# Compress stage of a hybrid decoder step: the first product over pairs of positions of one head, in two column groups

## The chip, the cores and the metric

The kernel runs on one core of one Trainium2 chip. The metric is the device time in microseconds (us) of one execution, from launch to the last output. The five engines of the core run programs of their own and meet at semaphores: TensorE (PE, its weight loads PEld), VectorE (DVE), ScalarE (ACT), GpSimd (POOL) and SyncE (SP), which here only issues DMAs.

## The reference, cut to what matters

One inference step of a one-layer decoder, for a prompt of 1024 tokens and 8 sequences that each add one token to 1024 cached ones. The part at issue is the compression of keys and values in the sparse attention heads. Cached raw keys and values lie in pages of 128 tokens, two heads of 64 elements side by side in a row of 128 numbers; a page table says which 8 pages a sequence has. Every block of 32 tokens of one head is flattened to 2048 numbers and goes through a small network:

```python
def compress(rows, pe, w1, w2):
    b, l, h, d = rows.shape
    nc = l // CMP_BLOCK                       # CMP_BLOCK = 32
    blocks = rows.reshape(b, nc, CMP_BLOCK, h, d) + pe[None, None, :, None, :]
    flat = blocks.transpose(0, 1, 3, 2, 4).reshape(b, nc, h, CMP_BLOCK * d)
    return jax.nn.silu(flat @ w1) @ w2        # w1 (2048, 64), w2 (64, 64)
```

It is done for keys and for values, over the 8 cached sequences (32 blocks each) and over the prompt (32 blocks), so over 9 x 32 = 288 blocks a head. The compressed keys are then normed. All is in float32.

## The kernel before

Four stages follow one another, with a barrier of all engines between them (`between`): `project` (input projection in 8 groups of columns, retention heads), `compress`, `attend_prompt`, `finish` (the 8 sequences and the output projection). A stage starts when every engine has left the one before. Inside a stage each engine's order of work is written out by hand; semaphores are counted, and nothing is planned at run time.

`project` works through column groups in the order qr, kr, vr, zr, q, wg, kv, zn, each for 8 tiles of 128 prompt rows and one tile of the 8 sample rows. Three pieces of it serve `compress`. In group kv, PE transposes the raw keys and values of each tile (L972) and DVE copies them to `kct` (L722), two of each a tile. In group zn, SP loads the 32 key pages of sequences 0 to 3 (L352) into `raw_a`. And SP loads the position vectors as single numbers, turned, into `pet` (L310, four DMAs).

`compress` (L1116 to L1378) goes through 16 units u: keys of sequences 0 to 7, then values. A unit is 8 pages, [128 tokens x 128] each. For each half unit i (4 pages), PE does 4 transposes of 128x128 into one of three PSUM banks (`turn_half`, L1328), after which head and element lie on the partitions and the token on the free axis. One copy of [128 x 512] then brings the half unit into `kcs` (`evacuate`, L1268 on DVE; for i = 1, 3, 5, 7 L1226 on ACT). It reads the bank in order and writes `kcs[:, position, block]` so that neighbouring numbers land 289 numbers apart. The page buffers are eight slots; SP issues pages 0 to 2, ACT pages 3 and 4, POOL pages 5 to 7 of each unit (L1163), values' pages after the keys' transposes have freed the slot.

The first product (`first`, L1347) is a sum over the 32 positions of a block: for each position one matmul with stationary weights of 128x128 (the 64x64 piece of w1 twice, for the two heads, on the diagonal, zeros elsewhere; DVE and POOL write the zeros, L1297 and L1204) and the moving columns of `kcs`. It runs in four parts: keys and values, each in a half of 128 columns (sequences 0 to 3) and a half of 161 (sequences 4 to 7, 32 blocks of the prompt, one column for the position vectors). Between every four positions PE turns one half unit of what is needed later. The prompt's columns come from `kct` by one DVE copy (L1257). Then come Silu on ACT (L1237), the second product (L1357), the key norms on DVE and POOL, and the transposes of the compressed keys (L1365).

Of the kernel before, what the change touches and what calls it, by code (L numbers as in the profile page):

```python
# [15 lines left out]
ACT = mybir.ActivationFunctionType  # L16
# [5 lines left out]
P = 128  # L22
D = 1024
T = 1024
# [109 lines left out]
def layout(nc, s):  # L134
# [21 lines left out]
    s.kct = m.put("kct", [P, 2, T])  # L156
# [17 lines left out]
    s.pet = tail.put("pe_t", [P, 2, CB])  # L174
    s.raw_a = Memory(nc, s.w_region).put("raw_pages_a", [P, FIRST, PAGES, P])
    s.c_first = [nc.alloc_semaphore(name=f"c_first{u}") for u in range(FIRST)]
# [11 lines left out]
def project(nc, s, io):  # L188
# [50 lines left out]
    with ExitStack() as ctx:  # L239
# [34 lines left out]
        def _(sp):  # L274
# [12 lines left out]

            load_x(0)
# [19 lines left out]
            for kv, pe_dram in enumerate((io["cmp_pe_k"], io["cmp_pe_v"])):  # L308
                for half in range(2):
                    sp.dma_start(pet[HD * half:HD * half + HD, kv, :],  # L310
                                 dram(pe_dram, 0, [1, HD], [HD, 32]),
                                 allow_slow_non_contiguous=True).then_inc(tables_in, 16)
            sp.dma_start(s.pages[:], io["page_table"].rearrange("(a b) p -> a (b p)", a=1)).then_inc(table_in, 16)
            for g in range(NG):
                if 1 <= g < NG - 1:
                    load_w(g + 1)
                for t in range(NT):
# [22 lines left out]
                    if kind == "zr":  # L340
                        sp.wait_ge(y_ready, t + 1)
                        to = io["y"][r0:r0 + n, 512:1024] if t < TT else dram(io["scratch"], O_ZR, [512, B], [1, 512])
                        sp.dma_start(to, s.st[0:n, slot, :]).then_inc(st_stored[slot], 16)
                    if kind == "zn" and t < 2 * FIRST:
                        if t == 0:
                            sp.wait_ge(table_in, 16)
                            sp.wait_ge(w_low, KT * (g + 1))
                        pool = io["cache_cmp_k"].rearrange("n t h d -> n t (h d)")
                        for p in range(4 * (t % 2), 4 * (t % 2) + 4):
                            at = PAGES * (t // 2) + p  # L350
                            page = sp.value_load(s.pages[0:1, at:at + 1], min_val=0, max_val=N_PHYS - 1)
                            sp.dma_start(s.raw_a[:, t // 2, p, :], pool[bass.ds(page, 1), :, :].rearrange("a t c -> (a t) c")).then_inc(s.c_first[t // 2], 16)  # L352
# [91 lines left out]
        turns_before = lambda kind, t: {"q": 2 * t, "wg": 2 * NT + t, "kv": 3 * NT + 2 * t}[kind]  # L444

        @block.scalar
        def _(act):
# [64 lines left out]
            def post(i):  # L512
# [4 lines left out]
                if kind in ("wg", "kv"):  # L517
                    br = 1 if kind == "wg" else 0
                    act.wait_ge(k_turned, b + (1 if kind == "wg" else 2))
# [91 lines left out]
        def _(dve):  # L611
# [100 lines left out]
            def post(i):  # L712
# [4 lines left out]
                if kind in ("wg", "kv"):  # L717
                    br = 1 if kind == "wg" else 0
                    if kind == "kv" and t < TT:
                        dve.wait_ge(k_turned, turns_before(kind, t) + 1)  # L720
                        for j in range(2):
                            own.step(nc.vector.tensor_copy(  # L722
                                view(s.kct[:, j, 4 * t:4 * t + 1], [1, 4], [32, 32]), view(s.ps[:, 3, P * j:P * j + 1], [32, 4], [1, 32])))
                        own.sync()
# [65 lines left out]
            for g in range(NG):  # L790
                for t in range(NT):
# [15 lines left out]
                    if i == 2 * NT:  # L807
                        dve.wait_ge(tables_in, 128)
# [39 lines left out]
        def _(pe):  # L848
# [103 lines left out]
            def post(i):  # L952
# [17 lines left out]
                if kind == "kv":  # L970
                    for j in range(2):
                        last = nc.tensor.transpose(s.ps[:, 3, P * j:P * j + n], st[:, KVW * j:KVW * j + KVW], one)  # L972
                    last.then_inc(k_turned, 1)
# [114 lines left out]
SLOTS, FIRST = 8, 4  # L1088
SP_PAGES, ACT_PAGES, POOL_PAGES = range(0, 3), range(3, 5), range(5, 8)

# [25 lines left out]
def compress(nc, s, io):  # L1116

    m = Memory(nc, s.x_region)
    w1 = m.put("w1_blocks", [P, 2, CB, P])
    raw_b = m.put("raw_pages_b", [P, SLOTS - FIRST, PAGES, P])  # L1120
# [9 lines left out]
    kcs = Memory(nc, s.w_region + 4 * FIRST * PAGES * P).put("kcs", [P, CB, ALL])  # L1130
    assert s.w_region + 4 * FIRST * PAGES * P + 4 * CB * ALL <= SB_END
    by_act = (1, 3, 5, 7)
    kept_a = lambda n: sum(1 for i in range(n) if i in by_act)
    kept_v = lambda n: n - kept_a(n)
    raw = lambda u: s.raw_a[:, u % SLOTS, :, :] if u % SLOTS < FIRST else raw_b[:, u % SLOTS - FIRST, :, :]
    pool_dram = [c.rearrange("n t h d -> n t (h d)") for c in (io["cache_cmp_k"], io["cache_cmp_v"])]
    with ExitStack() as ctx:
        sem = s.semaphore
        raw_in = [sem(f"c_raw_in{b}") for b in range(SLOTS)]
        raw_in_pool = [sem(f"c_raw_in_pool{b}") for b in range(SLOTS)]  # L1140
        w1_in, w2_in, zeroed = [sem(f"c_w1_in{kv}") for kv in range(2)], sem("c_w2_in"), sem("c_zeroed")
        cleared = sem("c_cleared")
        short_set, short_in, prompt_kept = sem("c_short_set"), sem("c_short_in"), sem("c_prompt_kept")
# [6 lines left out]

        OUT_BANK = [6, 7, 3]
# [4 lines left out]
        def load_pages(engine, u, some, loaded):  # L1156

            kv, b = u // B, u % B
            if u >= SLOTS:
                engine.wait_ge(turned, 2 * (u - SLOTS + 1))  # L1160
            for p in some:
                page = engine.value_load(s.pages[0:1, PAGES * b + p:PAGES * b + p + 1], min_val=0, max_val=N_PHYS - 1)
                engine.dma_start(raw(u)[:, p, :], pool_dram[kv][bass.ds(page, 1), :, :].rearrange("a t c -> (a t) c")).then_inc(loaded[u % SLOTS], 16)  # L1163

        def load_w1(engine, kv, half):
            at = slice(HD * half, HD * half + HD)
            engine.dma_start(w1[at, kv, :, HD * half:HD * half + HD],
# [1404 lines left out]
```

## Time and profile before

| | us |
|---|---|
| median of 3 runs | 987.76 (985.49, 987.76, 988.01) |
| span of the profiled execution, first to last instruction | 983.7 |
| the profiled execution's own time | not recorded; the median of the runs is 4.1 above the span |

| engine | busy us | share of the span | instructions |
|---|---|---|---|
| PE | 926.9 | 94% | 5293 |
| PEld | 705.9 | 72% | 5293 |
| DVE | 504.9 | 51% | 1079 |
| ACT | 314.3 | 32% | 699 |
| POOL | 191.3 | 19% | 235 |

`compress` runs from 486.6 to about 555.7 us of the span. Matmuls are pipelined, and the duration of a PE row holds the time through the array, so neighbouring rows overlap: the rate is read from start to start. One float32 matmul is two records in the trace, a transpose one.

### The profile page before, as it was taken

What the parts mean: (1) busy time and instruction counts of PE and PEld (TensorE: products, weight loads), DVE (VectorE), ACT (ScalarE), POOL (GpSimd) and SP (SyncE); (2) the same over time, 40 slices, a digit from 0 to 9 for tenths busy, and PEclk for the clock granted to TensorE, in tenths of its full rate; (3) what the DMA queues carried; (4) which work ended last, traced back from release to release, by engine and by line L of the source; (5) the groups of instructions that cost most, each with busy time, mean ns of one, the idle gap of its engine ahead of it and who ended that gap; (6) DMA issues with size and microseconds to landing.
All of it is one profiled execution on the core that took longest, in us unless ns stands there. A gap on an engine that the chain in (4) does not pass through costs nothing. (4 is left out here: it accounts for less than half of the span.)

```text
span 983.7 us, 15654 instructions
## 1 busy us (share of the span) xinstructions
PE 926.9 (94%) x5293; PEld 705.9 (72%) x5293; DVE 504.9 (51%) x1079; ACT 314.3 (32%) x699; POOL 191.3 (19%) x235
## 2 busy tenths in 40 slices
PE   7999989999999989999879998999999998999998
PEld 6676769998878777778579775666666665667784
DVE  4774253346344665450156357776666754564522
ACT  4222031223132334242110255555655553311100
POOL 1222222333102221110053102111011012343000
PEclk8999999999999999999979869999999999999999
DMA  7305811000621021312495410000000006788631
GB/s 263 132 17 117 213 42 46 2 1 1 233 115 49 22 65 47 106 43 94 114 207 154 104 47 22 22 22 22 1 22 1 22 18 219 225 224 294 207 103 48
DMA packets 90894, 91.13 MB, mean 93 GB/s; under 512 B 27630, under 2 KB 69534, under 8 KB 90454
## 3 DMA queue, kind: packets, MB, share of 16 engines
q1 hardware_dynamic: 70402, 71.60, 24.1%
q10 hardware_dynamic: 16700, 9.36, 3.5%
q0 software_dynamic: 3712, 9.17, 3.2%
q8 instruction: 43, 0.70, 0.3%
q14 instruction: 37, 0.30, 0.1%
HBM read 75.51 MB, written 23.49 MB: 101 GB/s over the span
## 5 line engine op out<-in xcount | busy, mean ns | idle before, releaser
L887 PE MATMUL ps<-w_high,x_high 128*128 128x512 f32 (+1 forms) x520 | 204.6, 393 | 2.3 <-DVE w_low L618 2.3
L889 PE MATMUL ps<-w_high,x_low 128*128 128x512 f32 (+1 forms) x520 | 199.8, 384 | 0.0
L888 PE MATMUL ps<-w_low,x_high 128*128 128x512 f32 (+1 forms) x520 | 199.3, 383 | 0.0
L887 PEld LDWEIGHTS ps<-w_high,x_high 128*128 128x128 f32 x520 | 98.1, 189 | 33.9 <-issue 12.9
L889 PEld LDWEIGHTS ps<-w_high,x_low 128*128 128x128 f32 x520 | 97.7, 188 | 20.9
L888 PEld LDWEIGHTS ps<-w_low,x_high 128*128 128x128 f32 x520 | 98.0, 188 | 18.9
L1718 PE MATMUL ps<-k_high,q_stack 128*128 128x512 f32 (+3 forms) x192 | 77.3, 406 | 12.1 <-DVE a_stats L1603 11.9
L399 POOL TENSOR_TENSOR stats<-stats,small 128x8 f32<-128x8 f32 (+3 forms) x35 | 41.7, 1190 | 213.9 <-DVE stats L670 159.3
L1718 PEld LDWEIGHTS ps<-k_high,q_stack 128*128 128x128 f32 x192 | 38.4, 200 | 53.2 <-DVE a_stats L1603 27.9
L1760 PE MATMUL ps<-weights_turned,v_nat 128*64 128x512 f32 x264 | 71.4, 622 | 0.0
L1719 PE MATMUL ps<-k_low,q_stack 128*128 128x512 f32 (+3 forms) x192 | 66.6, 354 | 0.0
L1268 DVE COPY kcs<-ps 128x512 f32<-128x512 f32 x28 | 30.3, 1084 | 62.6 <-PE ps L1328 62.5
L1512 POOL TENSOR_TENSOR y_tile<-y_tile,branch_out 128x512 f32<-128x512 f32 x15 | 19.1, 1276 | 221.5 <-DVEq L1661 221.5
L1603 DVE CUSTOM_DVE_ANT_1 window_logits<-ps,bias_full 128x640 f32<-128x640 f32 (+3 forms) x56 | 39.1, 709 | 34.0 <-PE ps L1719 33.7
L1533 ACT ACTIVATE full_logits<-full_logits,a_stats 128x128 f32<-128x128 f32 (+7 forms) x64 | 49.3, 771 | 20.8 <-DVE a_stats L1603 20.6
L1631 DVE COPY weights_turned<-ps 128x512 f32<-128x512 f32 x66 | 45.6, 690 | 18.8 <-PE ps L1739 14.3
L2359 PE MATMUL ps<-w_out_high,y_high 128*128 128x512 f32 x128 | 53.8, 420 | 1.4 <-DVE w_out_low L2086 1.4
L1542 ACT ACTIVATE weights_turned<-ps 128x512 f32<-128x512 f32 x66 | 39.0, 591 | 47.0 <-PE ps L1739 47.0
L456 ACT ACTIVATE w_high<-w_raw 128x512 fp32r<-128x512 f32 (+1 forms) x64 | 36.1, 601 | 54.6 <-PE ps L889 53.1
L1603 DVE CUSTOM_DVE_ANT_1 full_logits<-ps,bias_full 128x256 f32<-128x256 f32 (+6 forms) x56 | 45.0, 822 | 15.7 <-PE ps L1719 14.6
L2361 PE MATMUL ps<-w_out_high,y_low 128*128 128x512 f32 x128 | 50.2, 392 | 0.0
L2360 PE MATMUL ps<-w_out_low,y_high 128*128 128x512 f32 x128 | 50.0, 391 | 0.0
(340 smaller groups left out, 1597.9 us busy)
## 6 DMA issues: line engine op xcount, KB each, us to landing
w_raw<-in_w_in SPq DMA_DIRECT2D x48, 256.0 KB, 4.4
tmp_skew<-tmp_table SPq DMA_DIRECT2D x8, 576.0 KB
bias_full<-tmp_skew SPq DMA_DIRECT2D x8, 512.0 KB, 5.0
w_out_raw<-in_w_out SPq DMA_DIRECT2D x16, 256.0 KB, 4.7
y_rows_in<-tmp_y SPq DMA_DIRECT2D x8, 512.0 KB, 4.5
x_rows<-in_x_prompt SPq DMA_DIRECT2D x8, 512.0 KB, 5.6
out_y_prompt<-out_rows SPq DMA_DIRECT2D x8, 512.0 KB, 5.4
x_tile<-in_x_prompt SPq DMA_DIRECT2D x6, 512.0 KB, 3.9
```

The source lines that it names most:

```text
L887: nc.tensor.matmul(out, s.xh[:, k, rows], s.wh[:, k, 0:w], start=(k == 0), stop=False)
L888: nc.tensor.matmul(out, s.xh[:, k, rows], s.wl[:, k, 0:w], start=False, stop=False)
L889: ins = nc.tensor.matmul(out, s.xl[:, k, rows], s.wh[:, k, 0:w], start=False, stop=(k == KT - 1))
L1533: nc.scalar.activation(lg[:, h, 0:P * n], lg[:, h, 0:P * n], ACT.Exp, scale=-1.0, bias=st[:, S_MIN + H * j + h:S_MIN + H * j + h + 1], acc ...
L1603: nc.vector.tensor_tensor_reduce(out=columns(lg[:, h, 0:1]), in0=columns(pair[:, 0:1]), in1=view(full[:, TT - n, h, 0:1], [H * P, n], [1, ...
L1631: nc.vector.tensor_copy(pt[:, k % RP, 1, :], bank(k, 1)).then_inc(taken_v, 1)
L1718: nc.tensor.matmul(out, q(h), s.kh[:, j, h // G, k0 + c:k0 + c + w], start=True, stop=False)
L1719: last = nc.tensor.matmul(out, q(h), s.kl[:, j, h // G, k0 + c:k0 + c + w], start=False, stop=not (masked and c == 0))
L1760: last = nc.tensor.matmul(s.ps[at, 6, :], s.v[:, j, t + 1 - n + b, at], pt[:, k % RP, kv, :], start=(b == 0), stop=(b == n - 1))
L2359: nc.tensor.matmul(to, yh[:, t % 2, k, 0:n], wh[:, k, cols], start=(k == 0), stop=False)
L2360: nc.tensor.matmul(to, yh[:, t % 2, k, 0:n], wl[:, k, cols], start=False, stop=False)
L2361: last = nc.tensor.matmul(to, yl[:, t % 2, k, 0:n], wh[:, k, cols], start=False, stop=(k == KT - 1))
```

## The change

- Pages are loaded as pairs of tokens: one page goes to 64 partitions (a pair each) with 256 numbers a partition; two pages share a tile (`load_pages_paired`). A transpose of 128 columns then gives, for the even or the odd tokens, head and element on the partitions.
- A half unit i is now the even (i even) or odd tokens of a unit, and still 4 transposes. Its bank is brought to `kcs` by two copies of [64 x 512], one a head, that gather with steps of 16 numbers from PSUM and write runs of 32 neighbouring numbers. `kcs` has (parity, element) on its partitions, then head, pair of positions, block.
- The first product is over 16 pairs of positions: stationary weights 128x64 (`w1` as it is, no zeros to write), once for each head, the two heads' results in two column groups (PSUM partitions 0 to 63 and 64 to 127).
- The prompt is a ninth sequence (unit 8 and 17): its rows are read back from the output tensors by one DMA of 512 KB for the keys and one for the values. `kct`, its transposes and its copies go.
- The PSUM ring has four banks instead of three. DVE copies the half units 0 to 15 alone; from 16 on, ACT takes the odd ones. PE turns a whole unit after every three pairs of positions.
- Every unit from 6 on has a page buffer of its own. The pages of units 4 and 5 are loaded in `project`, in group q, into the place of `kct`. In `compress` 80 pages are loaded instead of 96. ACT issues all of its 20 pages before its first copy.
- The second product of the keys also waits for every copy (its banks are now in the ring).

```diff
+def load_pages_paired(engine, s, pool, b, some, tile, loaded):
+    for p in some:
+        page = engine.value_load(s.pages[0:1, PAGES * b + p:PAGES * b + p + 1], min_val=0, max_val=N_PHYS - 1)
+        at = HD * (p % 2)
+        engine.dma_start(tile[at:at + HD, p // 2, :], pool[bass.ds(page, 1), :, :].rearrange("a (r two) c -> (a r) (two c)", two=2)).then_inc(loaded, 16)
... (project)
+                    if kind == "q" and t < 2 * (EARLY - FIRST):
+                        if t == 0:
+                            sp.wait_ge(table_in, 16)
+                            sp.wait_ge(rows_in, 48)
+                            sp.wait_ge(r_out, TT)
+                        load_pages_paired(sp, s, pool, FIRST + t // 2, range(4 * (t % 2), 4 * (t % 2) + 4), s.raw_k[:, t // 2], s.c_first[FIRST + t // 2])
...
-                    for j in range(2):
-                        last = nc.tensor.transpose(s.ps[:, 3, P * j:P * j + n], st[:, KVW * j:KVW * j + KVW], one)
-                    last.then_inc(k_turned, 1)
... (compress)
-    w1 = m.put("w1_blocks", [P, 2, CB, P])
+    w1 = m.put("w1_pairs", [P, 2, CB // 2, HD])
-    by_act = (1, 3, 5, 7)
+    by_act = [i for i in range(4 * FIRST, 2 * n_u) if i % 2]
+        RING = 4
+        def load_prompt(engine, kv):
+            u = SEQS * kv + PROMPT
+            rows = io["prompt_out"][("cmp_k", "cmp_v")[kv]]
+            engine.wait_ge(turned, 2 * (kv + 1))
+            engine.dma_start(raw(u), dram(rows, 0, [2 * KVW, P], [2 * KVW * P, PAGES // 2], [1, 2 * KVW])).then_inc(raw_in[u], 16)
+        def kept_at(i, h):
+            b, at = i // 2 % SEQS, HD * (i % 2)
+            return kcs[at:at + HD, h, :, NBP * b:NBP * b + NBP]
+        def bank_of(i, h):
+            return view(s.ps[HD * h:HD * h + HD, i % RING, 0:1], [1, CB // 2], [CB // 2, NBP])
+        def may_keep(engine, i):
+            kv, b = i // 2 // SEQS, i // 2 % SEQS
+            if kv == 1:
+                engine.wait_ge(first_out, 1 if b < 4 else 2)
+            engine.wait_ge(turned, i + 1)
... (sync)
+            load_w1(sp, 0)
+            for u in paged[:2]:
+                load_pages(sp, u, SP_PAGES, raw_in)
+            load_prompt(sp, 0)
+            for u in paged[2:6]:
                 load_pages(sp, u, SP_PAGES, raw_in)
...
+            for u in paged[6:]:
                 load_pages(sp, u, SP_PAGES, raw_in)
+            load_prompt(sp, 1)
... (scalar)
+            for u in paged[:4]:
+                load_pages(act, u, ACT_PAGES, raw_in)
+            load_w1(act, 1)
+            for u in paged[4:]:
+                load_pages(act, u, ACT_PAGES, raw_in)
             for i in by_act:
+                may_keep(act, i)
+                for h in range(HKV):
+                    nc.scalar.activation(kept_at(i, h), bank_of(i, h), ACT.Copy).then_inc(evacuated_a, 1)
... (vector)
+            keep_position(0)
+            for i in range(2 * n_u):
+                if i == 2 * (SEQS + 4):
+                    keep_position(1)
+                if i not in by_act:
+                    may_keep(dve, i)
+                    for h in range(HKV):
+                        nc.vector.tensor_copy(kept_at(i, h), bank_of(i, h)).then_inc(evacuated, 1)
... (tensor)
+                for j in range(CB // 2):
+                    if then and j % 3 == 2:
+                        turn(then.pop(0))
+                    for h in range(HKV):
+                        last = nc.tensor.matmul(s.ps[HD * h:HD * h + HD, 4 + kv, cols], w1[:, kv, j, :], kcs[:, h, j, cols], start=(j == 0), stop=(j == CB // 2 - 1))
...
+            for u in range(FIRST):
+                turn(u)
+            first(0, 0, [4, 5, 6, 7, 8])
+            first(0, 1, [9, 10, 11, 12])
+            first(1, 0, [13, 14, 15, 16, 17])
+            second(0)
+            first(1, 1, [])
```

## Rows read from the trace of the kernel before

**Rows 1.** Busy time by stretch of compress: start:end length, engine (x instructions), clock, DMA share, GB/s
```profile
486.60:498.40 11.80, 5.91 (x36) 5.29 (x37) 8.28 (x8) 4.24 (x4) 5.59 (x9) 0.86 0.95 194
498.40:513.70 15.30, 12.06 (x94) 11.87 (x92) 8.71 (x8) 0.00 (x0) 9.16 (x13) 0.85 0.96 208
513.70:529.10 15.40, 15.15 (x96) 14.90 (x97) 8.83 (x10) 0.16 (x1) 7.57 (x14) 0.82 0.59 165
529.10:541.98 12.88, 11.74 (x103) 11.29 (x103) 9.49 (x11) 0.97 (x4) 2.81 (x6) 1.00 0.52 135
541.98:551.03 9.05, 9.05 (x67) 9.00 (x66) 2.55 (x12) 0.31 (x2) 2.09 (x3) 1.00 0.01 2
551.03:555.66 4.63, 2.93 (x16) 1.91 (x14) 1.68 (x6) 1.29 (x5) 0.01 (x1) 1.00 0.00 0
```

**Rows 2.** Timeline, PE in the first product: start, length, line, operation
```profile
504.98 0.60 PE L1328 MATMUL ps<-ident,raw_pages_b 128*128 128x128 f32 x4
505.41 1.06 PE L1347 MATMUL ps<-kcs,w_blocks 128*128 128x128 f32 x8
506.31 0.60 PE L1328 MATMUL ps<-ident,raw_pages_b 128*128 128x128 f32 x4
```

**Rows 3.** Waits in compress, PE for a DMA: total, times, longest
```profile
PE ps L1328 <- DMA raw_pages_a<-in_cache_cmp_v: 3.3, 1, 3.3
```

**Rows 4.** Timeline, PE in attend_prompt: two heads in two 64-wide column groups, and what follows
```profile
785.65 1.08 PE L1760 MATMUL ps<-weights_turned,v_nat 128*64 128x512 f32 x4
786.66 0.50 PE L1718 MATMUL ps<-k_high,q_stack 128*128 128x512 f32 x1
```

**Rows 5.** Groups of DVE instructions over the span, by shape: busy, mean ns, idle before
```profile
L1631 DVE COPY weights_turned<-ps 128x512 f32<-128x512 f32 x66 | 45.6, 690 | 18.8 <-PE ps L1739 14.3 <-DVE branch_out L1657 3.1 <-PE ps L1760 0.3
L1268 DVE COPY kcs<-ps 128x512 f32<-128x512 f32 x28 | 30.3, 1084 | 62.6 <-PE ps L1328 62.5
L2130 DVE TENSOR_REDUCE s_out_halves<-s_product 128x64 f32<-128x2048 f32 x1 | 3.7, 3731 | 0.0
```

**Rows 6.** Groups of ACT instructions over the span, by shape
```profile
L1542 ACT ACTIVATE weights_turned<-ps 128x512 f32<-128x512 f32 x66 | 39.0, 591 | 47.0 <-PE ps L1739 47.0
L510 ACT ACTIVATE q_stack<-ps,gain 128x512 fp32r<-128x512 f32 x16 | 10.2, 686 | 6.2 <-PE ps L962 6.1
L510 ACT ACTIVATE qfull<-ps,gain 64x32 f32<-64x32 f32 x2 | 0.6, 282 | 2.3 <-PE ps L988 2.3
L562 ACT ACTIVATE x_high<-ps 128x32 fp32r<-128x32 f32 x2 | 0.4, 198 | 6.5 <-PE ps L1001 6.4
L1226 ACT ACTIVATE kcs<-ps 128x512 f32<-128x512 f32 x4 | 4.2, 1113 | 9.5 <-issue 8.1 <-PE ps L1328 1.5
```

**Rows 7.** Timeline: four instructions back to back on DVE
```profile
843.15 2.49 DVE L2086 TENSOR_TENSOR w_out_low<-w_out_raw,w_out_high 128x512 fp32r<-128x512 f32 x4
```

**Rows 8.** Page loads of compress as issued by SP and ACT (timeline) and by POOL (by line)
```profile
518.73 12.82 SPq L1163 DMA_DIRECT2D raw_pages_b<-in_cache_cmp_v  x12
515.41 8.12 ACTq L1163 DMA_DIRECT2D raw_pages_b<-in_cache_cmp_v  x8
L1163 POOL DMA_DIRECT2D raw_pages_b<-in_cache_cmp_k x12: 547/547/954, 488.1 to 501.0; - x12
```

**Rows 9.** DMA issues from 486 to 560 us: KB each, median us from issue to landing
```profile
bias_full<-tmp_skew SPq DMA_DIRECT2D x6, 512.0 KB, 5.0
...
raw_pages_b<-in_cache_cmp_v SPq DMA_DIRECT2D x12, 64.0 KB, 2.3
```

**Rows 10.** Timeline, PE in group kv of project
```profile
407.61 0.38 PE L972 MATMUL ps<-ident,stage 128*128 128x128 f32 x2
407.83 0.38 PE L962 MATMUL ps<-ident,squares 128*128 128x128 f32 x2
```

**Rows 11.** Timeline, SP from 290 to 352 us: weight loads issued around group q
```profile
297.43 3.68 SPq L281 DMA_DIRECT2D w_raw<-in_w_in  x8
339.95 11.33 SPq L281 DMA_DIRECT2D w_raw<-in_w_in  x8
```

More of the change, by code:

```diff
@@ L518, in post @@
                     br = 1 if kind == "wg" else 0
[L519 removed]
+                    act.wait_ge(k_turned, b + 1)
                     if t < TT:
@@ L1156, in load_pages @@
         def load_pages(engine, u, some, loaded):
[L1158 to L1167, printed above, removed]
-                             dram(w1_dram[kv], 0, [HD, HD], [HD * HD, CB], [1, HD])).then_inc(w1_in[kv], 16)
@@ new lines, in turn @@
+            def turn(u):
+                landed(u)
+                for odd in range(2):
+                    i = 2 * u + odd
+                    if i >= RING:
+                        if i - RING in by_act:
+                            pe.wait_ge(evacuated_a, kept_a(i - RING + 1))
+                        else:
+                            pe.wait_ge(evacuated, kept_v(i - RING + 1))
+                    for q in range(PAGES // 2):
+                        last = nc.tensor.transpose(s.ps[:, i % RING, P * q:P * q + P], raw(u)[:, q, KVW * odd:KVW * odd + KVW], s.ident[:])
+                    last.then_inc(turned, 1)
@@ L1342, in first @@
-                pe.wait_ge(evacuated, kept_v(2 * B * kv + B * (half + 1)))
-                pe.wait_ge(evacuated_a, len(by_act))
-                for i in range(CB):
-                    if then and i % 4 == 0:
-                        turn_half(then + i // 4)
-                    last = nc.tensor.matmul(s.ps[:, 4 + kv, cols], w1[:, kv, i, :], kcs[:, i, cols], start=(i == 0), stop=(i == CB - 1))
+                    pe.wait_ge(w1_in[kv], 16)
+                else:
+                    pe.wait_ge(position_kept, kv + 1)
@@ L1366, in turn_keys @@
                 last.then_inc(key_turned, 1)
-            for i in range(B):
-                turn_half(i)
-            for kv in range(2):
-                for half in range(2):
-                    done = 2 * B * kv + B * (half + 1)
-                    first(kv, half, done if done < 4 * B else None)
-                    if kv == 1 and half == 0:
-                        second(0)
+            for u in range(FIRST):
[5 more added lines that the diff above has]
+            first(1, 1, [])
             turn_keys()
             second(1)
-            keep_clock(nc, s.ps[:, 0, 0:2 * P], w1[:, 1, 0, :], kcs[:, 0, 0:2 * P], 3)
+            keep_clock(nc, s.ps[:, 0, 0:2 * P], s.ident[:], kcs[:, 0, 0, 0:2 * P], 3)
 R_ = B * H
```

160 lines of the change are left out of this document (55 added, 105 removed).

## The prediction

> **What bounds the kernel now.** I read the table of stretches first, because the change touches one stage and a little of another. In compress, 486.6 to 555.7 us, PE is busy 57 of 69 us, DVE 40 [rows 1]. The stage falls into four kinds of time. At its start PE works half of the time and DVE, which copies what PE has turned, most of it: 8.3 of 11.8 us. Then PE works through products and transposes, with one gap waiting for pages, 3.3 us long [rows 3]. The reader is to see in [rows 1] that the two stretches around that gap have a mean clock of 0.85 and 0.82: PE fell to its lower level (1.2 of 2.4 GHz) behind each wait, and 15.4 us at 0.82 are 5.5 us at half speed, 2.8 us lost. From 514 us on PE is the bound: 15.2 of 15.4, 11.7 of 12.9, 9.05 of 9.05. Last comes a tail of 4.6 us of short dependent steps. A barrier ends the stage, so what the stage loses the run loses.
>
> **PE's prices.** A chunk of the timeline is four transposes from 504.98 to 505.41, 0.43 us, and four matmuls of 128 columns (eight records) to 506.31, 0.90 us [rows 2]: 0.225 us a matmul. With 161 columns it is 9.05 / 32 = 0.283 us [rows 1]. Before: 128 matmuls, 64 x 0.225 + 64 x 0.283 = 32.5 us, and 32 x 0.43 = 13.8 us of transposes.
>
> **Do two column groups of 64 run side by side?** The trace has that form: two heads, four records of 128x512 in 1.01 us, start to next start [rows 4]. At the rate of [rows 2] a record of 512 columns is 4 x 0.1125 = 0.45 us; one after another four make 1.80, side by side 0.90. So they run side by side, and 0.11 us is left. The products after are then 32 x 0.225 + 32 x 0.283 = 16.3 us; transposes 36 x 0.43 = 15.5 us. PE's sum falls by 14.5 us. I take the 0.11 as the price of going to the narrow form and back (bounds: 0, and 0.25 if all of the two latencies shows), 0.13 with a little for the wait of a transpose's data; there are 14 such returns, 1.8 us. The Trainium skill, TensorEngine Tiling (Array Packing), Key Properties, says that a change of tiling mode drains the array while a change of tile does not; the 0.11 us agrees with that, and at 14 returns it speaks against the change by under 2 us.
>
> **The copies.** Before: 32 copies of [128 x 512]. After: 72 of [64 x 512], 52 on DVE, 20 on ACT, each as long as one over 128 partitions. So the price of one decides the stage. The old copy takes 1084 ns on DVE and 1113 on ACT, where a copy of the same size with both sides in order takes 690 and 591 [rows 5, 6]: the scattered writing costs 400 to 520 ns. The new one writes in order and reads PSUM in steps of 16 numbers. No row of DVE shows such a read of PSUM. Lower bound 690 ns (L1631). Upper bound 1084: a DVE read of SBUF in steps of 64 costs 3731 ns for 2048 numbers [rows 5], 1.8 ns a number, just what the scatter costs. For ACT there is a row: L510 into `qfull` reads 32 numbers from PSUM in steps of 8, in 282 ns; a plain one takes 198 (L562), and the gain operand accounts for 686 - 591 = 95 [rows 6]. 198 + 95 = 293, so the step costs nothing there; at the scatter's 1.0 ns a number it would have shown 32 ns more. I take 690 on DVE too, as the same memory is read. Back to back four DVE instructions take 2.49 us, (2.49 - 0.69) / 3 = 0.60 each, 0.09 less than one alone [rows 7]. So I use 0.61 us a copy on DVE and 0.5 on ACT; at the other bound 1.0 on both.
>
> The Trainium skill, SBUF — State Buffer, Door 1: The DMA port swizzle, says that SBUF has lines of 16 bytes and PSUM of 8, that each access to a new line pays, and that any non-contiguous pattern in PSUM slows matmuls significantly. For SBUF the 1084 ns agree. For PSUM the ACT row does not, and for DVE nothing shows it; by the page the sum would be the first rival below.
>
> **The stage, step by step.**
> A. Start to first product. DVE alone copies half units 0 to 7: 487.3 + 0.2 (position column) + 16 x 0.61 = 497.4. Before: 498.4. The zero writing (3.5 us of DVE) is gone, and PE has four banks ahead, so nothing else is late.
> B. First product of the keys, first half. PE has only 16 x 0.225 + 5 x 0.86 + 0.65 = 8.6 us of work, but the next half waits for copies up to 17. DVE has 8 to 16: the first is ready at about 498.5, then 18 x 0.61 = 11.0; with 1 us for PE's transposes at the lower clock, 510.5. The copy of 17 is ACT's, which first issues 20 pages and a w1: 8 pages take 8.12 us [rows 8], so it is free at 488.5 + 21.1 = 509.6, done at 510.6. Before: 513.7. PE waits 2 us here in place of the 3.3 for pages, which are no longer reloaded into used slots.
> C. Second half. 16 x 0.283 + 4 x 0.86 + 4 x 0.13 = 8.5 us of PE, plus 2.4 for the lower clock behind the wait (2.8 before). DVE needs 1.22 and ACT 1.0 for what PE turns in 0.86 + 0.85, so PE leads. End 521.5, before 529.1.
> D. Values, first half. PE 8.6 us, to 530.1. But here the loads close in. SP's 12 pages take 12.82 us, POOL's 12.9 [rows 8]; 30 pages from 488.5 are 32 us, with 4 to 5 for the w1, w2 and prompt issues between, so the prompt's values are issued at 525. A DMA of 512 KB lands after 5.0 us [rows 9]: 530. Then 0.86 of transposes and 0.45 of product, and the last copies (0.2 + 1.2), for which the second product now waits: 532. Before: second product at 541.
> E. Second product 0.95, second half of the values 16 x 0.283 = 4.5: 537.5. The key norms, 4 us behind the second product, just fit. Before: 551.0.
> F. The tail is untouched, 4.6: 542.1 against 555.7.
> The stage gives back 13.5 us; I keep 13, for bubbles between turns that no row prices.
>
> **Project.** In group kv PE goes from matmul to matmul without a gap, and the two transposes L972 take 0.22 us of it, 407.61 to 407.83 [rows 10]: 8 x 0.22 and the two small ones, 1.8 us off the path. DVE's 16 copies of L722 go too; they lie beside PE and are worth nothing. Added are 16 page loads on SP in group q. SP has issued its weights by 301.1 and issues the next at 339.95 [rows 11]; 16 x 1.07 = 17 us fit. Its new waits are for work of the group before, and behind them stands only the weight load of 339.95; without that gap they would cost up to 17 us. Two position DMAs in place of four, half the w1 bytes: no one waits, 0.
>
> **Sum.** 983.7 - 13 - 1.8 = 968.9 of span, plus the 4.1 by which the median of the runs lies above the span: 973.
>
> **The rivals.**
> 1. The gather costs what the scatter did, on both engines. For: a step in SBUF does [rows 5]. Against: the ACT row, though of 32 numbers. A ends at 503.5, B at 523.7 (18 x 1.0), C at 534.6 or, if PE, which then works a third of the time, stays at the lower clock through it, at 541; D by DVE's five pairs of copies 10 us later, the last pair 2; E 5.5; F 4.6: 557 to 563. With -1.8 that is 987 to 993; as such waits lowered the clock each time before, I take 991: slower. It decides from about 0.95 us a copy.
> 2. DVE alone pays it. A and B are DVE's, so little is better: D is ACT's and PE's by half, end at 557, 987.
> 3. The narrow products run one after the other. B hides it, C is 4.5 later, D 2, E 4.5: +11, 984. Against it stand [rows 4].
> 4. Pages that go to 64 partitions, or the prompt rows, land late. From D on every us past 530 counts in full; a landing of 10 in place of 5 us makes 978. For: the DMA engines were at a share of 0.95 while three queues loaded pages [rows 1], and the 64 partitions may be reached by fewer of them. Against: a page landed in 2.3 us at the share of 0.5 to 0.6 that holds later [rows 9, 1], and it is now half as many pieces of twice the length.
> That a wider stall moves PE's clock in the next stage is within 3 us either way.
>
> **How the numbers follow.** Forecast 0.66 (968 to 978: gather 0.61 to 0.69 us, landings of 4 to 6, clock losses 0 to 3, the next stage), rival 1 0.11, rival 2 0.08, rival 3 0.04, rival 4 0.11. A difference under 0.3%, 3 us, can't be told from none. Faster: 0.66 + 0.11 + 0.02 of rival 3 + 0.02 of rival 2 = 0.81. Slower: 0.07 of rival 1. The same: 0.12. The range for 8 in 10 takes in rival 4 and reaches to rival 2: 967 to 987.
>
> **What would show it.** The copies at 0.69 (DVE) and 0.59 us (ACT), not near 1.1. Four product records of 128 columns in 0.225 us. Idle time of PE before the second half of the keys, released by a DVE or ACT copy, and before the last turn, released by the prompt's DMA. The stage 56 us long. In group kv two transposes fewer a tile. I am wrong if DVE's copies are over 0.9 us, if the stage is over 62 us, or if SP's later weight loads in project start after 341 us.

## The result and the profile after

Ten runs each: 981.48 us (978.74 to 984.75) in place of 986.48 (983.3 to 988.61). Ratio 0.9958, 95% interval 0.9940 to 0.9976: faster, by 5 us between the medians (4 by the ratio), where 14.8 were forecast. The profiled execution has a span of 981.5 us (before 983.7); its own time is 983.2, so a run takes 1.7 us more than its span. By that the profile of after lies 1.7 us above its median and the one of before 1.1 below its own, and the two spans differ by 2.2 only.

The table of stretches of compress, cut at the steps A to F of the prediction (PE, PEld, DVE, ACT, POOL busy, clock, DMA share, GB/s) [rows 1]:

```profile
489.13:501.85 12.72, 5.97 (x32) 5.10 (x33) 11.22 (x17) 0.00 (x0) 5.75 (x11) 0.77 0.79 197
501.85:518.70 16.85, 11.82 (x104) 9.20 (x105) 12.40 (x18) 1.20 (x2) 7.47 (x15) 0.80 0.85 195
518.70:530.10 11.40, 11.40 (x98) 9.02 (x98) 5.50 (x8) 4.80 (x8) 3.70 (x8) 0.80 0.33 95
530.10:541.27 11.17, 9.57 (x106) 7.66 (x105) 7.08 (x11) 6.67 (x12) 0.00 (x0) 1.00 0.61 161
541.27:546.75 5.48, 5.48 (x70) 4.93 (x71) 2.69 (x12) 0.77 (x3) 2.09 (x3) 1.00 0.01 3
546.75:551.95 5.20, 3.19 (x18) 2.11 (x16) 1.68 (x6) 1.29 (x5) 0.00 (x0) 1.00 0.01 2
```

The reader is to see two things. The stage starts at 489.13, 2.5 us later than before, though nothing of compress had begun. And the first two stretches, 29.6 us, have DVE busy for 23.6 and PE for 17.8, at a clock of 0.77 and 0.80; from 518.7 on PE is full. The stage takes 62.9 us in place of 69.0.

**Why it starts late.** First the end of project before, SP and ACT in the timeline, then the same after:

```profile
478.61 3.63 SPq L352 DMA_DIRECT2D raw_pages_a<-in_cache_cmp_k  x4
482.28 1.28 SPq L355 DMA_DIRECT2D tmp_zn<-stage  x2
...
482.61 0.59 ACT L475 ACTIVATE stage<-ps 8x512 f32<-8x512 f32 x1 [0.63 <-PE ps L879]
```

```profile
474.73 4.15 SPq L1090 DMA_DIRECT2D raw_pages_a<-in_cache_cmp_k  x4
478.92 0.58 SPq L356 DMA_DIRECT2D tmp_zn<-stage  x1
480.25 4.59 SPq L1090 DMA_DIRECT2D raw_pages_a<-in_cache_cmp_k  x4
484.89 0.99 SPq L356 DMA_DIRECT2D tmp_zn<-stage  x2
...
481.29 0.59 ACT L476 ACTIVATE stage<-ps 8x512 f32<-8x512 f32 x1 [1.51 <-DMA tmp_zn<-stage]
```

Before, SP issues a tile's pages and store in 4.86 us, and PE needs 5.55 a tile (ACT's copies are 5.55 apart); so SP, which starts group zn late, catches up, and its last store goes out as ACT's last copy ends. After, SP takes 5.52 us a tile (474.73 to 480.25): it never catches up, ACT waits 1.5 us for a store to land (before, its wait there was 0.63 us, and for PE), and the last two stores leave SP from 484.9 on. From the start of ACT's last copy to the next stage it is 7.8 us in place of 4.0.

**The copies.** The groups of compress, then DVE's timeline:

```profile
L1300 DVE COPY kcs<-ps 64x512 f32<-64x512 f32 x52 | 35.8, 689 | 14.3 <-PE ps L1333 13.0
...
L1245 ACT ACTIVATE kcs<-ps 64x512 f32<-64x512 f32 x20 | 12.0, 600 | 46.5 <-issue 35.5 <-PE ps L1333 10.8
```

```profile
490.25 11.50 DVE L1300 COPY kcs<-ps 64x512 f32<-64x512 f32 x16 [0.93 <-PE ps L1333]
504.06 12.97 DVE L1300 COPY kcs<-ps 64x512 f32<-64x512 f32 x18 [2.31 <-PE ps L1333]
```

689 and 600 ns, as long as a copy with both sides in order [rows 5, 6]: the read in steps is free. (The Trainium skill, SBUF — State Buffer, Door 1: The DMA port swizzle, gives PSUM lines of 8 bytes and says that a non-contiguous pattern there slows matmuls. For copies no such cost shows here: these read numbers 64 bytes apart and take as long as those in order.) But (11.50 - 0.69) / 15 = 0.72 us from start to start, not 0.61.

**The rest of the stage**, ACT and PE:

```profile
517.34 1.22 ACT L1245 ACTIVATE kcs<-ps 64x512 f32<-64x512 f32 x2 [35.46 <-issue]
...
518.70 1.34 PE L1350 MATMUL ps<-kcs,w_pairs 128*64 128x161 f32 x8 [4.69 <-ACT kcs L1245]
...
525.53 1.09 PE L1333 MATMUL ps<-ident,raw_pages_b 128*128 128x128 f32 x8
526.55 1.04 PE L1350 MATMUL ps<-kcs,w_pairs 128*64 128x161 f32 x12
527.52 1.09 PE L1333 MATMUL ps<-ident,raw_pages_b 128*128 128x128 f32 x8
...
541.27 1.02 PE L1362 MATMUL ps<-w_blocks,hidden 128*128 128x128 f32 x6 [1.60 <-ACT hidden L1250]
542.22 4.60 PE L1350 MATMUL ps<-kcs,w_pairs 128*64 128x161 f32 x64
```

ACT's first copy comes after its list of page loads, 1.5 us behind DVE's last (504.06 + 12.97 = 517.03), and PE waits 4.69 us. One load in that list is long, the first behind the DMA of `w1`; ACT's timeline from 500 to 503 us:

```profile
500.24 3.23 ACTq L1090 DMA_DIRECT2D raw_pages_b<-in_cache_cmp_v  x1
```

The median of ACT's page loads is 0.48 us. In the ten kernels below that keep this order it takes 2.0 to 3.1 us too.

A round of a turn and three pairs takes 525.53 to 527.52, 1.99 us; its parts alone are 0.86 + 3 x 0.283 = 1.71. The last half takes 4.5 us for 16 pairs, 0.283 each: the two heads run side by side.

### The profile page after: what moved, and what is told of

Same layout as the page of the kernel before. It is cut to its first block and busy times, and to the rows that moved or that the text cites. A ratio compares the mean times of both kernels' runs of the same rounds, so it can differ in the third digit from the quotient of the medians.

```text
span 981.5 us, 15674 instructions
## 1 busy us (share of the span) xinstructions
PE 915.1 (93%) x5291; PEld 686.9 (70%) x5291; DVE 501.2 (51%) x1083; ACT 321.9 (33%) x715; POOL 182.9 (19%) x227
## 5 line engine op out<-in xcount | busy, mean ns | idle before, releaser
L1537 ACT ACTIVATE window_logits<-window_logits,a_stats 128x640 f32<-128x640 f32 (+4 forms) x64 | 44.1, 689 | 18.4 <-DVE a_stats L1607 18.3
```

The costliest lines, as they stand in the source:

```text
L1537: nc.scalar.activation(lg[:, h, 0:P * n], lg[:, h, 0:P * n], ACT.Exp, scale=-1.0, bias=st[:, S_MIN + H * j + h:S_MIN + H * j + h + 1], acc ...
```

## The experiments

All are edits of the changed kernel. Medians are set against the kernel before on the same chip; kernels that ran once are read by their traces. Lengths of the stage run from its first transpose to attend_prompt's first matmul: 62.9 us in the changed kernel, and 61.4 to 62.9 in seven kernels whose stage is the same or came out the same (`plain_read`, `copy_as_scale`, `one_signal_a_pair`, `turned_order`, the two zn kernels, the changed kernel). So one trace tells lengths apart only beyond 1.5 us.

### Why compress starts late

```diff
# zn_old_form: group zn, SP
-load_pages_paired(sp, s, pool, t // 2, range(4 * (t % 2), 4 * (t % 2) + 4), s.raw_a[:, t // 2], ...)
+for p in range(4 * (t % 2), 4 * (t % 2) + 4):
...
+    sp.dma_start(s.raw_a[:, t // 2, p // 2, KVW * (p % 2):KVW * (p % 2) + KVW],
+                 pool[bass.ds(page, 1), :, :].rearrange("a t c -> (a t) c"))...
# zn_two_queues: SP keeps two pages a tile; the other two in POOL's loop
+if kind == "zn" and t < 2 * FIRST:
+    load_pages_paired(pool, s, cache_k, t // 2, range(4 * (t % 2) + 2, 4 * (t % 2) + 4), ...)
```

> Against the changed kernel only the 32 page loads in group zn of project differ: each goes to 128 partitions by 512 bytes again (the values of sequences 0 to 3 of the keys are then computed from wrongly placed rows). Theory A (the new form costs SP 468 ns an issue in place of 338 and its stores more as well, so SP and no longer PE sets the end of zn): an issue takes about 340 ns, the store 430, the last store leaves SP about 4 us earlier, compress starts at about 485.3 in place of 489.1, the run is about 4 us shorter than the changed kernel's 981.5 (977.5; 0.992 of the kernel before). Theory B (the start of compress came later for another reason, as DMA queues busy with the new lanes, or PE's clock): the issues get shorter but compress still starts at 488 to 489, and the time stays at 981.

> The changed kernel with the page loads of zn in the new form, but two of each tile's four issued by POOL, which has no work there. Theory A (SP's issue time is the bound): SP has 2 x about 1.04 + 0.6 us a tile, far below PE's 4.9; zn ends as PE allows, compress starts at about 485, the run at about 977.5 (0.992 of before). Theory B (the transfers themselves, into 64 partitions, hold up the weight or zn stores): same start as in the changed kernel, 489, time 981.

Measured: 975.97 us, ratio 0.9899 (0.9873 to 0.9925), and 976.48, 0.9897 (0.9872 to 0.9923). Compress starts at 482.8 and 484.95. SP in the first:

```profile
468.99 3.63 SPq L355 DMA_DIRECT2D raw_pages_a<-in_cache_cmp_k  x4
...
473.84 3.98 SPq L355 DMA_DIRECT2D raw_pages_a<-in_cache_cmp_k  x4
478.13 1.55 SPq L359 DMA_DIRECT2D tmp_zn<-stage  x2
```

and in the second:

```profile
470.00 1.72 SPq L1098 DMA_DIRECT2D raw_pages_a<-in_cache_cmp_k  x2
474.47 0.33 SPq L357 DMA_DIRECT2D tmp_zn<-stage  x1
475.55 1.71 SPq L1098 DMA_DIRECT2D raw_pages_a<-in_cache_cmp_k  x2
480.12 1.55 SPq L357 DMA_DIRECT2D tmp_zn<-stage  x2
```

4.85 us a tile of SP again, and in the second SP waits for PE's 5.55. From ACT's last copy to the next stage both have 4.1 to 4.2 us. In the eleven kernels with project as changed compress starts at 487.5 to 489.8 (mean 488.4), in the four with two queues at 483.0 to 485.0 (mean 483.8): 4.6 us. What lies ahead of group zn differs by over 2 us between executions, so it is cleaner to count from zn's first matmul to the first transpose of compress: 46.4 to 46.5 us in those eleven, 42.0 in the four with two queues, 41.8 in `zn_old_form` and in the kernel before. Theory A holds; the same bytes to the same 64 partitions in the second kernel rule out the transfers. So this alone took 4.5 to 4.7 us of what was forecast.

### The copies' distance, and which half of the partitions they touch

```diff
# plain_read: PSUM read in order
-return view(s.ps[HD * h:HD * h + HD, i % RING, 0:1], [1, CB // 2], [CB // 2, NBP])
+return view(s.ps[HD * h:HD * h + HD, i % RING, 0:1], [NBP, CB // 2], [1, NBP])
# copy_as_scale
-nc.vector.tensor_copy(kept_at(i, h), bank_of(i, h)).then_inc(evacuated, 1)
+nc.vector.tensor_scalar(kept_at(i, h), bank_of(i, h), 1.0, None, ALU.mult).then_inc(evacuated, 1)
# one_signal_a_pair: .then_inc(evacuated, 2) behind the second copy only
# same_partitions: read the half that is written
-s.ps[HD * h:HD * h + HD, i % RING, 0:1]
+s.ps[HD * (i % 2):HD * (i % 2) + HD, i % RING, 0:1]
# turned_order
-for h in range(HKV):
+for h in ((0, 1), (1, 0))[i % 2]:
```

> The changed kernel with the 72 copies of turned tokens reading PSUM in order in place of steps of 16 numbers (so each product takes the wrong columns). Theory A (the step is free; the 0.72 us from start to start is what any DVE instruction with a PSUM source takes back to back): mean 688 ns and 0.72 us apart as now, ACT 600 and 0.61, stage the same 62.9 us. Theory B (the step costs a little, hidden in the distance between starts): 16 copies in 9.8 us in place of 11.5, stretch A ends 1.7 us earlier, B about 2.

> The changed kernel with DVE's 52 copies written as a multiplication by 1.0 (TENSOR_SCALAR) in place of COPY; the result is the same. Theory A (COPY is what starts 0.72 us apart; two L829 TENSOR_TENSOR of 128x512 out of PSUM take 1.29 us together, 0.60 apart, in the same trace): 16 copies take 9.7 us in place of 11.5, A ends 1.8 and the second half of the keys starts about 1.5 to 2 us earlier (then ACT's copy of half unit 17, at 517.3, is the last); stage 1.5 to 2 us shorter, time about 979.5. Theory B (any one-source read of PSUM by 64 partitions, or the semaphore that each copy sets, gives 0.72): nothing changes, 981.5.

> The changed kernel with DVE signalling once behind each pair of copies in place of behind each copy; the result is the same. Theory A (the signal keeps the next copy from starting inside the last 0.1 us of the one before): pairs take 1.29 us in place of 1.41, the first copy of a pair no longer costs 0.72; 16 copies 10.6, stretch A 0.9 us shorter. Theory B (it lies in the access, not in the signal): 1.41 and 11.5 stay.

> The changed kernel with each DVE and ACT copy reading the same 64 partitions that it writes (so one head's products are computed from the other head's columns or its own twice). Theory A (0.72 us from start to start because a copy moves between partition halves, or because consecutive copies read different halves): 16 copies take 9.7 us in place of 11.5, stretch A 1.8 us shorter. Theory B (it lies elsewhere, in the signal after each copy or in the runs of 32 numbers that it writes): 0.72 stays.

> The changed kernel with DVE's two copies of each odd half unit in the other order (head 1 first). In stretch A successive pairs then read the same half of the partitions across the border of pairs and write another; inside a pair the half that is read changes and the half that is written does not, as before. The result is the same. Theory A (a change of the half read makes 0.72 us of 0.60, whatever is written): 16 copies take 0.69 + 8 x 0.72 + 7 x 0.60 = 10.65 us in place of 11.5. Theory B (a change of either half, read or written, does it): 11.5 stays.

Measured: `plain_read` 16 copies in 11.50 us; `copy_as_scale` 11.49, median 981.26, ratio 0.9949 (0.9933 to 0.9965), no gain over the changed kernel; `one_signal_a_pair` copies start at 490.91, 491.61, 492.33, 493.03, about 0.71 apart; `turned_order` 11.49. Only `same_partitions` moved. DVE's timeline there:

```profile
488.92 10.55 DVE L1300 COPY kcs<-ps 64x512 f32<-64x512 f32 x16 [0.93 <-PE ps L1333]
501.78 11.86 DVE L1300 COPY kcs<-ps 64x512 f32<-64x512 f32 x18 [2.31 <-PE ps L1333]
519.38 1.28 DVE L1300 COPY kcs<-ps 64x512 f32<-64x512 f32 x2 [5.74 <-PE ps L1333]
```

A pair takes 1.28 us in place of 1.41: 0.60 from start to start while both copies keep to one half of the partitions. From pair to pair the half changes, and 8 x 0.60 + 7 x 0.72 + 0.69 = 10.5 is just what 16 take. ACT's pairs fell from 1.22 to 1.08 too. `turned_order`, whose pairs meet on the half that is read but not on the one written, gained nothing, so a change of either side costs the 0.12 us. From pair to pair the PSUM bank changes too, and the copy has a wait in front of it, but neither makes the 0.12: two DVE instructions in project read two banks over all partitions, with a wait between them, and start 0.60 apart (timeline of the changed kernel):

```profile
157.60 1.29 DVE L829 TENSOR_TENSOR scores<-ps,decay 128x512 f32<-128x512 f32 x2
```

My first three theories (step, kind, signal) fell; `same_partitions` gave half of what its theory A expected (0.95 us of 1.8), as the change from pair to pair stayed; the last of the five was Theory B of its run. Against the 0.61 of the prediction this is an estimate of 34 x 0.11 = 3.7 us in A and B; no run has all its copies 0.60 apart. And as the copies stand each pair must change halves on the side it reads; another layout was not tried.

### ACT's late copy, its late Silu, and copies shared from the start

```diff
# w1_by_sp: load_w1(sp, 1) behind SP's 18th page in place of load_w1(act, 1)
# silu_early: in ACT's loop over by_act
+if i == 27:
+    hidden(0)
# share_from_start (w2 loads moved behind the prompt's values)
-by_act = [i for i in range(4 * FIRST, 2 * n_u) if i % 2]
+by_act = [1, 3, 5, 7] + [i for i in range(26, 2 * n_u) if i % 2]   # the first four ahead of ACT's loads
```

> The changed kernel with the load of w1 for the values issued by SP behind its first 18 pages in place of by ACT behind its first eight. Theory A (ACT's list of issues, 27.3 us, makes its copy of half unit 17 the last thing before the second half of the keys): ACT is free 0.9 to 1.3 us earlier, the copy ends at about 517.3 in place of 518.6, the second half starts with DVE's last copy, at 517.2 to 517.5; stage 1.2 us shorter. Theory B (ACT's issues wait on the DMA queues, not on their number): ACT's 20 page loads end at 517 all the same, under 0.3 us gained.

> The changed kernel with ACT's Silu of the keys ahead of its last five pairs of copies in place of behind them. Theory A: the second product no longer waits for hidden; it follows DVE's or ACT's last copy, idle time of PE ahead of it 0.8 to 0.9 in place of 1.6 us, stage 0.7 to 0.9 us shorter. Theory B (PE's transposes then wait for ACT's copies, which come 0.7 us later through the whole stretch): nothing gained.

> The changed kernel with ACT copying half units 1, 3, 5, 7 ahead of its page loads and DVE taking all of half units 8 to 25; w2 is loaded behind the prompt's values. Theory A (DVE's 0.72 us a copy bounds the first product of the keys): stretch A ends after 5.8 us of DVE in place of 11.5, about 496; DVE then ends half unit 17 at about 511 (before 518.7 with ACT's late copy), second half 522 to 523, the last prompt rows land near 531 to 534 and the second product starts at 535 to 536 in place of 541.3; stage end 546 to 547 in place of 552.0, time about 976 (0.990 to 0.991 of before). Theory B (PE's lower clock after the gaps, or landings of ACT's pages, which now start 5 us later, bound it): second product not before 539, gain under 2 us.

Measured: stage 61.8, 61.7 and 61.8 us, none of which can be told from no gain; `share_from_start` 980.74 us, 0.9947 (0.9927 to 0.9968), no better than the changed kernel. What moved shows inside the stage. In `w1_by_sp` the second half of the keys comes 27.95 us after the stage's start, now released by DVE; it is 29.57 in the changed kernel and 28.8 to 29.4 in seven others whose edit leaves that part alone. The longest of ACT's twenty loads is now 0.99 us. In `silu_early` the second product waits 1.02 us for a copy in place of 1.60 for `hidden`:

```profile
516.74 1.34 PE L1350 MATMUL ps<-kcs,w_pairs 128*64 128x161 f32 x8 [3.12 <-DVE kcs L1300]
```

```profile
538.76 1.02 PE L1368 MATMUL ps<-w_blocks,hidden 128*128 128x128 f32 x6 [1.02 <-ACT kcs L1253]
```

Both theories A hold for what PE waits for. The gains are some 1.2 us at the start of the second half, and 0.6 us of wait; that the stage keeps them shows only in `small_steps` below. Sharing the copies moved much and kept little:

```profile
496.25 0.66 PE L1355 MATMUL ps<-kcs,w_pairs 128*64 128x128 f32 x8 [1.78 <-ACT kcs L1241]
...
512.00 1.34 PE L1355 MATMUL ps<-kcs,w_pairs 128*64 128x161 f32 x8 [4.56 <-issue]
...
526.58 0.66 PE L1355 MATMUL ps<-kcs,w_pairs 128*64 128x128 f32 x8 [2.87 <-issue]
```

From the stage's start, A ends after 8.0 us (12.7 in the changed kernel) and B after 23.7 (29.6), as expected; but C takes 14.6 us in place of 11.4. Its clock is 0.55 in 510 to 515 us and 0.77 to 520, behind a wait of 4.6 us, and DVE, which has all of C's copies, is the last. Of 5.9 us won 3.2 go there, and D, at 0.75 in 525 to 530, takes 1.6 more. The second product starts at 539.3, as theory B said, and not at 535 to 536: behind the first half of the keys, theory A failed.

### The change of form, and the column groups

```diff
# turns_in_halves
-if then and j % 3 == 2:
-    turn(then.pop(0))
+if then and j % 3 == 1:
+    turn(then[0], (0,))
+if then and j % 3 == 2:
+    turn(then.pop(0), (1,))
# one_column_group
-last = nc.tensor.matmul(s.ps[HD * h:HD * h + HD, 4 + kv, cols], ...)
+at = 0 if j else HD * h
+last = nc.tensor.matmul(s.ps[at:at + HD, 4 + kv, cols], ...)
```

> The changed kernel with every turn inside a first product cut in two: half its transposes after position 1, half after position 2 of each three. Nothing is added but 14 more changes from 64-column to 128-column form and back. Theory A (each excursion costs PE 0.30 us in products and transposes): in the second half of the keys, where PE leads, four more excursions make 1.2 us, 11.4 to 12.6 us; a turn of four transposes and the four records behind it stand 0.15 above a plain row each. Theory B (it was not the change of form but waits for bank and pages): the stretch grows by under 0.4 us, and the two half turns together cost what one did.

> The changed kernel with both heads' products (from the second position on) sent to the same 64 columns of PE, so the sums of the two heads run together. Theory A (the two heads' records run side by side only since they go to different column groups): a pair of 161 columns takes 0.55 to 0.57 us in place of 0.283; the last product, 16 pairs in 4.60 us, takes 8.8; C 4.2 us longer, D 3.4 longer, B hides it behind the copies; stage 12 us longer, 994. Theory B (a 64-column product costs half by itself): the last product stays at 4.6 us.

Measured: with the turns in halves, a round at full clock, PE's timeline:

```profile
524.41 0.77 PE L1353 MATMUL ps<-kcs,w_pairs 128*64 128x161 f32 x8
525.11 0.66 PE L1334 MATMUL ps<-ident,raw_pages_b 128*128 128x128 f32 x4
525.69 0.49 PE L1353 MATMUL ps<-kcs,w_pairs 128*64 128x161 f32 x4
526.12 0.66 PE L1334 MATMUL ps<-ident,raw_pages_b 128*128 128x128 f32 x4
526.71 0.77 PE L1353 MATMUL ps<-kcs,w_pairs 128*64 128x161 f32 x8
```

524.41 to 526.71 is 2.30 us, against 1.99: 0.3 us for one excursion more, and C and D together take 25.6 in place of 22.6, 3.0 for nine more. Theory A holds: an excursion costs 0.3 us. (The Trainium skill, TensorEngine Tiling (Array Packing), Key Properties, says that a change of tiling mode drains the array. The trace agrees, and the price of 0.3 us is the trace's.) With one column group the last half:

```profile
543.95 8.69 PE L1351 MATMUL ps<-kcs,w_pairs 128*64 128x161 f32 x64
```

8.6 us to the next start in place of 4.5: theory A on the form. The stage is 70.3 us, 7.4 longer, not 12: C and D grew by 4.5 only, where 7.6 were expected, and A and B were 1.2 shorter. Part of it is the clock. The wait before C was short, and PE ran C at full clock, where the changed kernel has 0.80:

```profile
515.88 1.00 PE L1351 MATMUL ps<-kcs,w_pairs 128*64 128x161 f32 x8 [1.30 <-DVE kcs L1300]
```

```profile
515.88:530.00 14.12, 14.12 (x106) 12.34 (x107) 5.70 (x9) 4.80 (x8) 4.36 (x9) 1.00 0.33 94
```

The 11.4 us of C at 0.80 are 2.3 us lost, so about 2 of the missing 3.1 are a clock loss that this kernel does not have. The rest is open.

### Versions with the losses taken out

```diff
# small_steps = zn_two_queues + w1_by_sp + silu_early
# balanced = zn_two_queues + silu_early, and
+by_act = [i for i in range(2 * n_u) if i % 2]
+for i in (1, 3, 5, 7):
+    keep(i)
+for u in paged[:2]:
+    load_pages(act, u, ACT_PAGES, raw_in)
+for k in range(2, 10):
+    keep(2 * k + 5)
+    load_pages(act, paged[k], ACT_PAGES, raw_in)      # page loads: SP 33, ACT 14, POOL 33
# balanced_loads: the same, SP 30, ACT 19, POOL 31, w1 of the values by SP
```

> The changed kernel with zn's page loads on two queues, and in compress ACT copying every odd half unit from the start with its 14 page loads between the copies (SP and POOL 33 each), the prompt's values ahead of the last three sequences, w2 last, the Silu early. Theory A (copies are DVE's bound only while ACT issues loads; PE and the page issues are the floor): A 6 to 7 us, B 11, C 9.5 to 10.5, second product at about stage start + 47 (now + 52.1), stage end 57 us after its start in place of 62.9; with zn's 5 us the run is 971 (0.985 of before). Theory B (gaps that PE has between A and B lower its clock, and what A and B give, C loses, as when the copies were shared at the start alone): stage 60 to 61 us, run 974 to 975 (0.988).

> The changed kernel with three steps that each alone did what was expected: zn's page loads on two queues, w1 of the values loaded by SP, Silu of the keys early. If they add: compress starts at about 484.3, is 62.9 - 1.2 - 0.8 = 60.9 us long; the run is 4.3 + 2 = 6.3 us shorter than the changed kernel's, 975 (0.989 of before). If PE's clock takes the small ones back: 977.

> As the balanced kernel (ACT copies every odd half unit, zn on two queues, Silu early), but with page loads 30 on SP, 31 on POOL, 19 on ACT in place of 33, 33 and 14, as PE waited for pages six times there. Theory A (the issue of page loads is the bound, 3.5 us a sequence in place of 4.0): second product at stage start + 45 to 46 in place of 49.8, stage 56 us, run 971 (0.985 of before). Theory B (ACT, with 19 loads of about 1.1 us and 18 pairs of copies of 1.22, is now the bound): B 4 us longer, the second product at + 49, no gain.

| | median us | ratio to before, 95% | stage |
|---|---|---|---|
| changed kernel | 981.48 | 0.9958 (0.9940 to 0.9976) | 62.9 |
| small_steps | 975.36 | 0.9898 (0.9873 to 0.9924) | 60.2 |
| balanced | 976.67 | 0.9909 (0.9893 to 0.9925) | 60.1 |
| balanced_loads | 972.81 | 0.9863 (0.9839 to 0.9887) | 58.6 |

`small_steps` is what was expected; its ratio can't be told from that of zn_two_queues, its stage can. In `balanced` A and B are over 16.95 us after the start (changed kernel 29.6), and then PE waits for pages six times:

```profile
500.34 0.77 PE L1378 MATMUL ps<-kcs,w_pairs 128*64 128x161 f32 x8 [0.81 <-ACT kcs L1258]
505.67 1.09 PE L1361 MATMUL ps<-ident,raw_pages_b 128*128 128x128 f32 x8 [2.57 <-DMA raw_pages_b<-in_cache_cmp_v]
...
525.03 1.97 PE L1361 MATMUL ps<-ident,raw_pages_b 128*128 128x128 f32 x8 [2.78 <-DMA raw_pages_b<-in_cache_cmp_v]
...
533.22 1.02 PE L1390 MATMUL ps<-w_blocks,hidden 128*128 128x128 f32 x6 [0.99 <-ACT kcs L1258]
```

The stage is as long as in theory B, but the cause is not the clock, which stays at 1.00 from the stage's start to 520 us: it is the page loads, for which PE waits 10.6 us in all:

```profile
PE ps L1361 <- DMA raw_pages_b<-in_cache_cmp_v: 10.6, 6, 2.8
```

Shifting five of them to ACT, which now takes a pair of copies every 2.43 us with two issues between, leaves four such waits of 5.4 us in all, for the same bytes, and brings the second product to start + 48.3 (49.8 in `balanced`, 52.1 in the changed kernel):

```profile
502.74 0.77 PE L1378 MATMUL ps<-kcs,w_pairs 128*64 128x161 f32 x8 [3.70 <-ACT kcs L1260]
...
526.78 1.09 PE L1361 MATMUL ps<-ident,raw_pages_b 128*128 128x128 f32 x8 [1.39 <-DMA raw_pages_b<-in_cache_cmp_v]
...
531.27 1.02 PE L1390 MATMUL ps<-w_blocks,hidden 128*128 128x128 f32 x6 [0.99 <-ACT kcs L1260]
```

That is the fastest version here, 12.7 us below the kernel before in the same comparison (985.46); both theories had half of it (B longer by 2.8 us, as theory B says, the waits shorter, as theory A says). What it could not keep is the clock: behind the 3.70 us of wait PE has 0.76 to 510 us and 0.79 to 518.

## Why the prediction was wrong

The direction was right, and none of the rivals came: the step of the read is free (rivals 1 and 2), the narrow products run side by side (rival 3), no landing was late (rival 4). The size was off, 5.0 in place of 14.8 us: 981.5 lies outside the 968 to 978 of the likeliest case, and the stage, at 62.9 us, is over the 62 that the prediction gave as a sign of being wrong. That 981.5 is inside the wide range of 967 to 987 is luck, as that range was drawn for rivals 2 and 4. By the prediction's steps, in us of the span:

| step | forecast | measured | shown by |
|---|---|---|---|
| project, ahead of group kv | 0 | -0.4 | not the change's: that point moves by over 2 us between executions |
| project, group kv | -1.8 | -1.8 (62.04, then 60.26 us; 60.2 to 60.3 in all sixteen kernels) | traces |
| project, group zn | 0 | +4.7 (41.80, then 46.47 us) | two runs |
| A | 10.8 | 12.7 | 16 copies 0.72 apart: 1.7 |
| B | 13.2 | 16.9 | copies: 2.0; ACT's copy late: 1.6 |
| C | 10.9 | 11.4 | excursions 0.30, not 0.13: 0.7 |
| D | 10.5 | 11.2 | PE and a late Silu, not the prompt's landing |
| E, F | 10.1 | 10.7 | |
| kept for bubbles | 0.5 | | |
| behind compress | 0 | +1.5 (428.0, then 429.5) | not shown |

- Right: the 1.8 us of group kv, counted from the two matmuls with `to_rows` just ahead of group kv's tiles (382.82 and 382.40) to zn's first matmul (444.86 and 442.66); the 16 loads moved to group q (SP issues them in 19.3 us from 300.6, and its next eight weight loads are out by 349.8, before by 351.3); E.
- The step that failed first is one that the prediction doesn't have. It counted the 16 loads that move to group q, and put the 32 in group zn at nothing without a reason, though their form changed too. But 64 partitions by 1 KB cost SP 469 ns an issue where 128 by 512 bytes cost 338, and the store behind them 584 in place of 431. SP had 0.7 us a tile to spare; four loads and a store took it. The two runs that undo it, by the form or by a second queue, give 4.5 to 4.7 us back.
- "I use 0.61 us a copy on DVE" went by a row of SBUF work over all partitions [rows 7]. Copies that change from half to half start 0.72 apart. That is 3.7 us by estimate, the largest mis-sized term of the stage. (Its upper bound, of which nothing came, has a reading that is loose: 1.8 ns a number is not "just what the scatter costs", which is 1084 / 512 = 2.1.)
- "The copy of 17 is ACT's, done at 510.6": the 21.1 us of ACT's issues were 27.3. Two things make most of the 6.2 us. The new form costs here too: an issue takes ACT 484 ns where 345 was the median before, 2.8 us over twenty loads. And the load behind `w1` took 3.23 us, 2.7 more than the others; `w1_by_sp` shows that it goes with `w1`. Its copy ended 1.5 us behind DVE's last, which was itself late.
- The landing of the prompt's values, on which D was built, was no bound: SP issued it at 530.3, it took 4.0 us, and PE turned it from 537.99 on without a wait. Since A and B took 5.6 us more, D was PE's, and the second product waited for ACT's Silu, which the prediction never placed.
- The 0.13 us of an excursion was read from one row [rows 4] that shows one way only, behind long records; the way there and back costs 0.3.
- The term 4.1 was the distance of a median of three from one span. A run takes 1.7 us more than its span; the other 2.4 was this execution's luck, and the profile of after lies on the other side. That is why the two spans differ by 2.2 and the medians by 5.
- The 1.5 us behind compress stay open. The same stretch took 427.6 to 433.1 us in the kernels run here, none of which changed it, so it is within what executions differ by.

## What to carry to other kernels

A DMA that only changes its shape has a new price on the queue that issues it: recount the queue's time per tile against the engine that sets the pace, and look at how much it has to catch up. When copies are split over halves of the partitions, price them from a row that alternates halves too. And when one engine's stretch is shortened, ask at once what comes second: here it was a list of page loads, issued one by one, for which PE then waited 10.6 us. Before a stage's gain is read from a single trace, see how much that stage moves where nothing in it was changed: here 1.5 us, more than two of the edits were worth.

## What the runs showed of the hardware

- DMA issue on SP: 469 ns for 64 partitions by 1 KB, 338 ns for 128 by 512 bytes; a store of 256 KB just behind 584 and 431 ns. On ACT 484 and 345 ns.
- On ACT, the page load behind the `w1` load: 2.0 to 3.2 us in eleven kernels, against a median of 0.48; with `w1` on SP the longest is 0.99.
- DVE and ACT, copies of 64 x 512: 0.60 and 0.48 us from start to start within one half of the partitions, 0.72 and 0.62 when the half read or written changes (pairs of 1.28 and 1.08, and 1.41 and 1.22 us, less 0.69 and 0.60).
- PE, going from 64-column to 128-column form and back: 0.3 us.
- PE, float32 in two groups of 64 columns: a pair of 161 columns every 0.283 us, in one group every 0.54.
